# Normalising the window attention's probabilities on POOL instead of VectorE, in one queue with the solve's masks

## What is computed

```python
# window attention: 8 query heads, 2 key/value heads, blocks of 128 queries, 256 keys each
scores = einsum(q, k_band) * d ** -0.5                # masked to the window
m = maximum(scores.max(-1), sink)
p = exp(scores - m)
denom = p.sum(-1) + exp(sink - m)
out = einsum(p / denom, v_band)

# delta rule: A strictly lower triangular per chunk
T = triangular_solve(eye + A, eye)
U, W = T @ (v * beta), T @ (k * beta * exp(G))        # then a scan over the chunks
```

## Time and profile before

| | |
|---|---|
| median of 3 runs | 3922.81 us (3914.93 to 3922.91) |
| the profiled execution | 3916.69 us, its span 3914.9 us |
| mean granted clock of TensorE in it | 0.963 |
| PE busy | 3731.1 us (95%) |
| DVE busy | 2220.9 us (57%) |
| ACT busy | 1275.7 us (33%) |
| POOL busy | 724.9 us (19%) |

### The profile page before, as it was taken

The page is one execution under the profiler, slowest core; times in us unless marked ns, Lnnn a source line. Parts: engine busy times, 40 slices in busy tenths (PEclk is TensorE's granted clock), DMA queues, the critical chain, the costliest instruction groups (busy, mean ns, idle before and its releaser), DMA issues. The chain is left out here.

```text
span 3914.9 us, 42324 instructions
## 1 busy us (share of the span) xinstructions
PE 3731.1 (95%) x16750; PEld 2879.0 (74%) x16750; DVE 2220.9 (57%) x3018; ACT 1275.7 (33%) x1829; POOL 724.9 (19%) x434
## 2 busy tenths in 40 slices
PE   8999998999999999998999989888999999989999
PEld 6888733888878888535888876685888767867887
DVE  6545546754474445457645576675444657755443
ACT  3222234522242223334422344424222343343221
POOL 3432001343213430001434023120000020200000
PEclk9999998999999999998999999798999998989999
DMA  4443200433324342102433322002222220012222
GB/s 170 139 139 103 96 22 18 142 135 136 114 97 136 123 140 81 58 23 86 137 135 132 94 81 60 1 1 65 92 93 101 81 72 21 1 49 82 94 98 81
DMA packets 92948, 345.44 MB, mean 88 GB/s; under 512 B 10832, under 2 KB 11088, under 8 KB 91856
## 3 DMA queue, kind: packets, MB, share of 16 engines
q1 hardware_dynamic: 92752, 342.74, 26.2%
HBM read 340.60 MB, written 2.10 MB: 88 GB/s over the span
## 5 line engine op out<-in xcount | busy, mean ns | idle before, releaser
L381 ACT ACTIVATE w_hi<-raw 128x1024 fp32r<-128x1024 f32 (+2 forms) x540 | 561.0, 1040 | 1905.7 <-PE ps L325 1892.4
L323 PE MATMUL ps<-xs_hi,w_hi 128*128 128x512 f32 x2472 | 980.5, 397 | 35.4 <-DVE xs_lo L542 16.3
L324 PE MATMUL ps<-xs_lo,w_hi 128*128 128x512 f32 x2472 | 969.5, 392 | 0.0
L325 PE MATMUL ps<-xs_hi,w_lo 128*128 128x512 f32 x2472 | 968.8, 392 | 0.0
L391 DVE TENSOR_TENSOR w_lo<-raw,w_hi 128x1024 fp32r<-128x1024 f32 (+2 forms) x540 | 667.4, 1236 | 127.0 <-ACT w_hi L381 126.7
L323 PEld LDWEIGHTS ps<-xs_hi,w_hi 128*128 128x128 f32 x2472 | 468.1, 189 | 161.2 <-issue 33.7
L325 PEld LDWEIGHTS ps<-xs_hi,w_lo 128*128 128x128 f32 x2472 | 468.4, 189 | 98.8
L324 PEld LDWEIGHTS ps<-xs_lo,w_hi 128*128 128x128 f32 x2472 | 468.8, 190 | 98.0 <-issue 3.6
L323 PE MATMUL ps<-hd_hi,w_hi 128*128 128x512 f32 x1320 | 527.3, 399 | 3.5 <-DVE hd_lo L484 3.5
L324 PE MATMUL ps<-hd_lo,w_hi 128*128 128x512 f32 x1320 | 524.3, 397 | 0.0
L325 PE MATMUL ps<-hd_hi,w_lo 128*128 128x512 f32 x1320 | 524.1, 397 | 0.0
(11 more groups left out here) (447 smaller groups left out, 4339.6 us busy)
## 6 DMA issues: line engine op xcount, KB each, us to landing
raw<-in_ffn_gu SPq DMA_DIRECT2D x264, 512.0 KB, 3.6
arena<-in_ada SPq DMA_DIRECT2D x64, 768.0 KB, 5.5
raw<-in_ffn_dn SPq DMA_DIRECT2D x96, 448.0 KB, 3.3
raw<-in_in_t SPq DMA_DIRECT2D x60, 512.0 KB, 3.6
raw<-in_ffn_dn SPq DMA_DIRECT2D x48, 512.0 KB, 3.5
raw<-in_out SPq DMA_DIRECT2D x32, 512.0 KB, 3.6
raw<-in_pleg SPq DMA_DIRECT2D x16, 512.0 KB, 3.6
raw<-in_in_r SPq DMA_DIRECT2D x8, 512.0 KB, 3.8
```

The costliest lines, as they stand in the source:

```text
L323: T.matmul(bank, lhs_hi(k), rhs_hi(k), start=(first and k == 0), stop=False)
L324: T.matmul(bank, lhs_hi(k), rhs_lo(k), start=False, stop=False)
L325: mm = T.matmul(bank, lhs_lo(k), rhs_hi(k), start=False, stop=(last and k == kt - 1))
L381: A.activation(self.hi[:, n % HL, 0:size], raw[:, n % RAW, 0:size], ACT.Copy).then_inc(self.high_done, 1)
```

## The change

The four multiplications leave `window_dve` and become `window_pool`, on POOL. DVE no longer waits for its reciprocal; the reciprocal counts a new semaphore `inv_ready`, for which POOL waits. POOL's list is woven from `delta_pool`, which first yields five times and then once per mask (not after mask 0), and `window_pool`, by the same `weave`.

```diff
-            masked, probs_ready = st.sem("masked"), st.sem("probs_ready")
+            masked, probs_ready, inv_ready = st.sem("masked"), st.sem("probs_ready"), st.sem("inv_ready")
...
                         order.done(V.tensor_tensor(w_inv[:, g, :], w_total[:, g, :], w_esink[:, g, :], ALU.add))
-                        order.done(V.reciprocal(w_inv[:, g, :], w_inv[:, g, :]))
+                        V.reciprocal(w_inv[:, g, :], w_inv[:, g, :]).then_inc(inv_ready, 1)
+                    yield
+
+            def window_pool(pool):
+                for m in range(11):
+                    if 1 <= m < 9:
+                        g = m - 1
+                        pool.wait_ge(inv_ready, g + 1)
                         for q in range(ST):
-                            V.tensor_scalar(sc[g % 3][:, q, :], sc[g % 3][:, q, :], w_inv[:, g, q:q + 1], None, ALU.mult) \
+                            G.tensor_scalar(sc[g % 3][:, q, :], sc[g % 3][:, q, :], w_inv[:, g, q:q + 1], None, ALU.mult) \
                              .then_inc(probs_ready, 1)
                     yield
...
-            @st.block.gpsimd
-            def _(pool):
+            def delta_pool(pool):
+                for i in range(5):
+                    yield
                 pool.wait_ge(head_ready, 8)
                 G.memset(state, 0.0).then_inc(zeroed, 1)
                 for i, (v, hd) in enumerate(turns):
...
                      .then_inc(low_ready, 1)
+                    if i:
+                        yield
+
+            @st.block.gpsimd
+            def _(pool):
+                weave(delta_pool(pool), window_pool(pool))
```

## The result

Twenty runs of each kernel: before 3918.87 us in the median (3909.02 to 3924.99), the change 3926.64 us (3914.30 to 3933.42). The ratio is 1.0018 with a 95% interval of 1.0011 to 1.0026, so 7 us more (4 to 10). The profiled execution of the change took 3917.84 us, 8.8 us under the median of its twenty runs and 1.2 us over the profiled execution of the kernel before: the profile shows the mechanism, and not the whole of the 7 us.

A forecast was written before the change was run, and what follows sets the result against it. TensorE, without gaps in the window turns, was taken to bound the kernel. VectorE's relief counted nothing; waits for POOL, 3.6 + 2.2 = 5.8 us, on the median of 3922.8 gave 3928.6 us, range 3914 to 3940.

The forecast's parts named there:

- I cost the gain at nothing: Window turns: the 18.2 us of multiplications leaving VectorE only lengthen its wait for TensorE, so 0 us gained.
- Rival (a): Window turns: VectorE sets the pace, so 14 x 1.06 = 14.8 us less, 3908; chance 0.08.
- The price of one multiplication: One 128x256 tensor_scalar on POOL: estimated at 910 ns from the 128x512 and 128x768 rows, bounds 734 and 1556 ns.
- The time of one normalisation: Four multiplications on POOL, 3.64 us, plus 1.2 us held by VectorE's L2803 or L2814: 4.85 us from the reciprocal's end.
- Covered: Masks queued on POOL behind the normalisations: still ready before TensorE reads them, by under 2 us for masks 2 and 3; cost nothing.
- The forecast's 0.5 us at L2803: Pair 3, both layers: POOL's last multiplication stands in the way of VectorE's second L2803, costing half an instruction, 0.5 us.
- The waiting transposes: TensorE's transposes (L2374) wait for POOL's longer normalisation: 3.6 us in layer 0, 2.2 us in layer 1.
- Pair 1 was forecast 1.4 us late: Layer 0: POOL's normalisation ends at 2490.6, TensorE wants the transposes at 2489.18, so 1.4 us late; layer 1 in time.
- Rival (c): Pair 1's new gap, layer 0: TensorE's clock falls at once, 5.8 + 4.8 = 10.6 us more, 3933.4; chance 0.27.
- The forecast wanted the stretch: Sign: from first masked scores to the solve's last turns, 3 to 4 us longer in layer 0, 2 in layer 1.
- The sum of 5.8 us: Whole kernel: 3.6 us of layer 0 plus 2.2 us of layer 1 late; 3928.6 us against the median of 3922.8.

The follow-up runs named there:

- POOL busy beside it, nobody waiting: Nothing normalised, against the kernel before; POOL makes four 128x256 multiplications per pair into tensors nobody reads, at the change's queue places: 0.9995, 2.0 us less.
- its twin on the other base: The kernel before, VectorE still normalising, plus four POOL multiplications of 128x256 per pair into tensors nobody reads: 1.0011 against the kernel before, 4.3 us more.
- POOL's work doubled: The change plus four POOL multiplications per pair into tensors nobody reads, ahead of the four that normalise: 1.0066 against the kernel before, 25.9 us more.
- half and half: The change with two of each pair's four normalising multiplications on VectorE and two on POOL: 0.9996 against the kernel before, 1.6 us less.

## Why the forecast held, and where it did not

The differences of the medians from the kernel before:

```
nothing normalised, nothing on POOL                    -6.7 us  (-11 to -2)
POOL busy beside it, nobody waiting   -2.0 - (-6.7) =  +4.7 us  (-2 to 11)
the transposes waiting for POOL       +7.1 - (-2.0) =  +9.1 us  (4 to 14)
the change                                             +7.1 us  (4 to 10)
```

The first and the third are clear of zero, the second is not; its twin on the other base (4.3 us) has VectorE's multiplications beside it, and TensorE's waits show that the two bases are not alike.

Beside these, the profiles: VectorE's turns (us from a pair's reciprocal to the next one's, layer 0 / layer 1), and the sum of TensorE's idle entries from the transposes of pair 0 to those of pair 7, both layers together.

| kernel | pair 4 to 5 | pair 5 to 6 | TensorE idle | more than before | time, measured |
|---|---|---|---|---|---|
| before | 6.56 / 6.57 | 6.94 / 6.98 | 10.8 | | |
| the change | 6.71 / 6.49 | 9.37 / 6.49 | 13.6 | +2.8 | +7.1 |
| without normalisation | 5.44 / 5.43 | 6.50 / 8.13 | 10.7 | -0.1 | -6.7 |
| the same, POOL busy | 6.70 / 6.70 | 6.84 / 6.70 | 11.1 | +0.3 | -2.0 |
| before, POOL busy | 7.22 / 7.22 | 7.22 / 7.21 | 15.4 | +4.6 | +4.3 |
| pairs 0 to 3 on POOL | 6.57 / 6.56 | 6.98 / 6.99 | 12.5 | +1.7 | +2.7 |
| pairs 4 to 7 on POOL | 6.70 / 6.70 | 8.13 / 9.09 | 15.1 | +4.3 | +7.8 |
| POOL's work doubled | 10.09 / 6.62 | 7.93 / 13.41 | 30.6 | +19.8 | +25.9 |
| half and half | 6.27 / 6.27 | 6.26 / 7.28 | 12.5 | +1.7 | -1.6 |
| six pairs on ScalarE | 5.37 / 5.37 | 10.69 / 10.66 | 14.2 | +3.4 | +5.1 |

The idle time is of one execution, the time of the median of many. Apart from the run without normalisation the last two columns stay within about 6 us of each other; what is left between them no run separates, and TensorE's clock is the one thing that is seen to move.

**"I cost the gain at nothing" held for the waits, and not for the time.** The step was that VectorE's freed time becomes a longer wait for TensorE. The rows without any normalisation show just that: VectorE's turn is 1.12 us shorter, TensorE's waits are the same 5.8 us. Rival (a), that VectorE sets the pace, is not borne out by them. Still, that kernel is 6.7 us quicker, and its runs lie at a higher granted clock. The forecast had no term for this, and no run shows its mechanism. VectorE's turn is nearly full all the same: where POOL's work was added to it (7.22 us), TensorE did wait.

**The price of one multiplication held.** 910 ns was estimated, 918 at the least and 925 in the median measured. **The time of one normalisation was oversized where it mattered.** 4.85 us from the reciprocal's end was forecast, 4.06 and 4.37 measured at pairs 1 and 4. At pair 1 the first of the four took 1.27 us and the others ran at their usual pace; at pair 4 the first took 1.27 and the second 1.21. Pair 0, beside the scan L2796 that the forecast left out, took 5.2 us in both layers, where nobody waited for it.

**"Covered" held for the masks, by another way than thought.** In the change they fall on L2444 and L2449 and stretch them by 1.34 us in layer 0; the time is covered, as VectorE's wait of 3.34 us behind them shows. The forecast's 0.5 us at L2803 is not there: in both layers the second one behind pair 3 (L2810 in the change) began right behind its predecessor and took its 0.69 us.

**The waiting transposes were the right mechanism, mis-sized and in part misplaced.** The forecast had 5.8 us: 3.6 in layer 0, 2.2 in layer 1. The subtraction gives 9.1, the idle time in the profile 2.8 (1.3 and 1.5). Pair 1 was forecast 1.4 us late in layer 0; in the profile of the change it was on time, because TensorE's scores ran at half clock in that execution (granted 0.50 from 2484 to 2489; 0.69 from 2485 to 2489 in the kernel before). The run with pairs 0 to 3 on POOL shows the lateness (0.41 to 0.97 us) where the clock is full. Pair 4 waits 2.4 us for POOL in place of 1.13 for ScalarE, in layer 0 of the change and in both layers of the run with pairs 4 to 7; in layer 1 of the change pairs 3 to 5 wait 1.70, 0.98 and 0.78.

**Rival (c), the clock, is part of it, at pair 4 and not at pair 1.** TensorE by stretch, first the kernel before, then the change (length, busy, granted clock, DMA share, GB/s), each from shortly before pair 4's transposes:

```profile
2514.00:2518.00 4.00, 3.65 (x18) 0.60 0.01 4
2518.00:2524.00 6.00, 6.00 (x42) 0.98 0.00 0
```

```profile
2513.00:2517.00 4.00, 1.72 (x8) 0.92 0.01 2
2517.00:2523.00 6.00, 5.87 (x26) 0.50 0.01 3
```

Before, TensorE was back at 2.4 GHz by about 2518, behind 1.13 us of idle time; in the change it idled for 2.41 us and stayed at 1.2 GHz from 2517 to 2523. From pair 3's transposes to pair 5's it took 16.86 us in place of 14.29. Of these 2.57 us the longer wait is 1.28, and 1.27 lie between the transposes of pairs 4 and 5, where nothing waits: that is the clock. VectorE's two turns from pair 4 to 6 are longer by the same 2.58 us, which leaves nothing for the stretched instructions. The wait does not settle the clock by itself: behind the same 1.13 us the clock was half in the kernel before and full without normalisation, and in layer 1 of the change it stayed full.

**How much of the agreement is luck.** The forecast wanted the stretch 3 to 4 us longer in layer 0 and 2 in layer 1. From pair 0's transposes to pair 7's the profile has 5.7 us more in layer 0 (64.86 against 59.13) and 4.8 less in layer 1 (57.10 against 61.91), the second with more idle time than before: the clock moves a layer by more than the change does. The sum of 5.8 us counted waiting alone, and had about twice what the profile shows of it; the rest of the measured 7.1 us is not in any wait that the profile shows, and the clock, which the forecast had left to a rival, is what is seen to move. How much of the 9.1 us is waiting and how much the clock is not separated by these runs.

## To carry to other kernels

A shorter turn on one engine is no gain yet: look whether the wait of the next engine has become shorter. Here leaving a work out took 1.12 us from VectorE's turn and nothing from TensorE's waits. And look where the profiled execution lies among the runs: the change's was 9 us under its median, the one without normalisation 12 us over, so neither shows the difference of the medians. For work moved to POOL there are three prices: its own longer duration before the reader, what VectorE loses beside it, and where the instructions queued behind it on POOL come to lie. The first follows from a step between two sizes in the trace; the other two can be looked for by letting POOL do the work into a tensor that nobody reads. In this kernel the first is the one that TensorE waited for.

## What was not expected of the hardware

Very small VectorE instructions were held by a POOL instruction for the rest of its duration: L2449, 128x4, took 1.13 us in place of 0.15 and ended with the mask beside it, and L2444, a tensor_scalar of 128x4 with an operand from SBUF, took 0.59 in place of 0.23. The kernel before has it too, at pair 7, where L2449 took 0.80 us beside a mask. A row maximum over 1024 columns and an eviction from PSUM beside POOL's multiplications and masks kept 1.22 and 1.28 us. And the spread of this program's runs goes with the granted clock: among the change's twenty, the mean clock ranges from 0.959 (3933.4 us) to 0.966 (3917.8 us), with a correlation of -0.86 between clock and time.
